# The matmuls on constants at three inner seams of a two-layer trunk are left out

## What is computed

```
def hybrid_layer(x, ...):
    h = rms_norm(x, g_mix_pre)
    proj = h @ w_in
    ...                                   # three attention branches, gated and added: mixed
    x = x + rms_norm(mixed @ w_out, g_mix_post)
    h = rms_norm(x, g_mlp_pre)
    u = jnp.square(jax.nn.relu(h @ w_up))
    return x + rms_norm(u @ w_down, g_mlp_post)
```

## Time and profile before

| what | value |
|---|---|
| median of 3 runs | 1807.53 us (1807.1 to 1808.18) |
| the profiled execution's own time | 1808.27 us |
| its span, first to last instruction | 1806.5 us |
| TensorE busy | 1763.2 us, 98% of the span |
| VectorE, ScalarE, GpSimd busy | 1057.9, 827.1, 145.0 us |
| mean granted clock of TensorE | 0.992 |
| chain that ended last | TensorE 86%, VectorE 7%, ScalarE 3% |

### The profile page before, as it was taken

One profiled execution on the slowest core, in us unless ns is written; L12 is line 12 of the kernel. 1 busy time (PEld: TensorE's weight loads), 2 busy tenths in 40 slices (PEclk: granted clock), 3 DMA queues, 4 the chain that ended last, 5 costly groups with the idle time before them and its releaser, 6 DMA issues.

```text
span 1806.5 us, 20939 instructions
## 1 busy us (share of the span) xinstructions
PE 1763.2 (98%) x8298; PEld 1450.1 (80%) x8298; DVE 1057.9 (59%) x1378; ACT 827.1 (46%) x1115; POOL 145.0 (8%) x140
## 2 busy tenths in 40 slices
PE   8999999999999999999999999999999999999996
PEld 6887888888878888888778878888888788888884
DVE  7877775654547534354487777655554664343544
ACT  7575555555345414131366755655544353231221
POOL 0111121111100000000001112111111000000000
PEclk9999999999999999999999999999999999999998
DMA  4121112222332222222221221122224132222221
GB/s 149 65 78 59 59 59 71 70 67 74 122 99 93 93 95 94 94 93 94 93 99 62 74 70 48 59 71 71 71 82 136 62 117 94 93 94 93 96 95 66
DMA packets 46609, 152.30 MB, mean 84 GB/s; under 512 B 5296, under 2 KB 7728, under 8 KB 46512
## 3 DMA queue, kind: packets, MB, share of 16 engines
q1 hardware_dynamic: 44784, 147.29, 24.5%
q10 hardware_dynamic: 1728, 3.67, 0.5%
HBM read 146.75 MB, written 4.19 MB: 84 GB/s over the span
## 4 chain that ended last, share of the span: by engine, by line
PE 86%; DVE 7%; ACT 3%; issue 2%; DMA 0%; POOL 0%; DVEq 0%; SPq 0%; ACTq 0%
PE bank L475 79%; PE bank L480 4%; PE bank L741 1%; PE bank L701 1%; DVE hf L1422 1%; DVE x L1429 1%; DVE w_lo L1378 1%; DVE h_lo L1411 1%; ACT w_hi L891 1%; DMA trig<-in_trig 0%; ACT dn L943 0%; ACT dn L941 0%; PE bank L551 0%; DVE mx L1472 0%; PE bank L496 0%
## 5 line engine op out<-in xcount | busy, mean ns | idle before, releaser
L475 PE MATMUL bank<-h_hi,w_hi 128*128 128x512 f32 x1248 | 493.3, 395 | 12.0 <-DVE h_lo L1411 10.5
L475 PE MATMUL bank<-h_hi,w_lo 128*128 128x512 f32 x1248 | 488.3, 391 | 0.0
L475 PE MATMUL bank<-h_lo,w_hi 128*128 128x512 f32 x1248 | 488.1, 391 | 0.0
L891 ACT ACTIVATE w_hi<-raw 128x1024 fp32r<-128x1024 f32 (+2 forms) x275 | 277.1, 1012 | 223.1 <-DMA raw<-in_w 222.6
L1378 DVE TENSOR_TENSOR w_lo<-raw,w_hi 128x1024 fp32r<-128x1024 f32 (+2 forms) x275 | 324.6, 1183 | 60.6 <-ACT w_hi L891 54.6
L475 PEld LDWEIGHTS bank<-h_hi,w_hi 128*128 128x128 f32 x1248 | 235.8, 189 | 66.2 <-issue 10.3
L475 PEld LDWEIGHTS bank<-h_hi,w_lo 128*128 128x128 f32 x1248 | 235.4, 189 | 49.9
L475 PEld LDWEIGHTS bank<-h_lo,w_hi 128*128 128x128 f32 x1248 | 235.7, 189 | 47.8 <-issue 1.4
L475 PE MATMUL bank<-u_hi,w_hi 128*128 128x512 f32 x512 | 203.1, 397 | 0.0
L475 PE MATMUL bank<-u_lo,w_hi 128*128 128x512 f32 x512 | 203.1, 397 | 0.0
L475 PE MATMUL bank<-u_hi,w_lo 128*128 128x512 f32 x512 | 203.1, 397 | 0.0
(11 more groups left out here) (239 smaller groups left out, 2547.4 us busy)
## 6 DMA issues: line engine op xcount, KB each, us to landing
raw<-in_w SPq DMA_DIRECT2D x257, 512.0 KB, 3.3
x<-in_x SPq DMA_DIRECT2D x16, 256.0 KB, 3.8
x_spill<-x ACTq DMA_DIRECT2D x8, 256.0 KB, 2.0
x<-x_spill SPq DMA_DIRECT2D x8, 256.0 KB, 3.4
out_y<-x SPq DMA_DIRECT2D x8, 256.0 KB, 2.0
raw<-in_w SPq DMA_DIRECT2D x8, 192.0 KB, 2.4
raw<-in_w SPq DMA_DIRECT2D x8, 128.0 KB, 2.3
raw<-in_first ACTq DMA_DIRECT2D x1, 768.0 KB, 8.8
```

The lines of the kernel that those rows point to most:

```text
L475: mm = pe.matmul(o, s, m, start=start and i == 0 and j == 0, stop=last and i == n - 1 and j == 2, skip_group_check=True)
L891: act.activation(w_hi[:, gc % RING, 0:w], raw[:, gc % RING, 0:w], ACT.Copy).then_inc(whi.sem, 1)
```

## The change

The two calls of `keep_warm(WARM)` and the constant are taken out. The warm-up at the start of the program (14 matmuls) stays. No wait is added or removed, and no other engine's program changes; TensorE issues 84 matmuls less in an execution, 28 at each of the three seams.

```
@@ -26,7 +26,6 @@
 GROUPS = D_FF // D
 
 RING = 4
-WARM = 28
 
 
 def order():
@@ -867,7 +866,6 @@
                     for t in range(KT):
                         tile(("out", t), mix_hi, mix_lo, (mix_l, 0) if t == 0 else None)
                     norm_sum(POST)
-                    keep_warm(WARM)
 
                     up(0)
                     for g in range(GROUPS):
@@ -875,8 +873,6 @@
                             up(g + 1)
                         down(g)
                     norm_sum(MPOST)
-                    if now[0] + 1 < DEPTH:
-                        keep_warm(WARM)
 
             @block.scalar
             def _(act):
```

## The result

The changed kernel took 1810.14 us (median of 20 runs, 1808.31 to 1811.63) and the kernel before 1807.31 us (median of 20, 1806.26 to 1808.49): a ratio of 1.0014 with a 95% interval of 1.0008 to 1.0020. It is slower by 2.8 us (1.4 to 3.6 by the interval). The profiled execution took 1810.25 us, 1.98 us more than that of before.

The account below looks back on a forecast made before the run. TensorE, busy 98% of the span, was taken as the bound. Constants 0.0, three slow starts of 1.95 us, less three waits of 0.60, gave + 4.05 us on 1807.53: 1811.6 us, range 1809.2 to 1814.2.

Parts of the forecast that it names:

- The constants stand beside the chain, not on it: At the three seams, constants end before the norm chain delivers input and do not slow it; removal directly gains 0.0 us.
- The clock falls at all three seams: TensorE idles about 7.6 us at each seam, so its clock is at 1.2 GHz when `three_tiles` starts.
- The price of a slow start, 1.95 us less 0.60: At each seam the first ten matmuls take 4.32 us, not 2.37; less a vanished wait, net 1.35 us.
- The wait at the fifth tile: In `three_tiles` at each seam, TensorE's 0.60 us wait for `h_lo` disappears when TensorE starts late.
- the prediction's formula: Slow-start cost at a seam with n slow matmuls: 0.30 + (n - 1) x 0.197 + 0.08 us.
- both rivals on the length of the start: At each seam: about six slow matmuls, 2.3 us in all, chance 0.10; or 14, 7.0 us in all, chance 0.13.
- I take nothing off: After the seams the whole chain moves along with TensorE, so the rest of the program swallows none of the 4.05 us.
- the row at 948.30: After the layer boundary, TensorE waits 0.91 us for VectorE work that had itself waited for TensorE.
- the fall in layer 1 lost: Rival: a clock fall in the attention goes away, saving 1.7 us, total 1809.9 us; chance 0.10.
- the opposite, one fall more, is as possible: In the attention, one extra clock fall is as possible as a lost one, and lies inside the forecast's own range.
- the rival's 1809.9: Total in us if an attention clock fall goes away: + 4.05 - 1.7 = 2.35 us; chance 0.10.
- a loss of over 0.2%: Whole kernel slower by more than 3.6 us, the least a measurement can tell from no change; chance 0.64.

Follow-up runs that it names:

- both attempts to move the pause: Against the kernel before: 42 constants at the layer boundary, 1807.43 us against 1807.79; bare boundary plus 8 constant matmuls ahead of layer 1's attention pause, 1809.26 against 1808.32.
- the last trace: Boundary constants removed and 8 constant matmuls added ahead of layer 1's attention pause, against the kernel before: 1809.26 us against 1808.32, ratio 1.0006.

## Why the prediction was right, and where it was not

**The constants stand beside the chain, not on it: right.** The 20.9 us of TensorE's time that they took are worth nothing. The chain takes 8.72 us with them and without.

**The clock falls at all three seams: right.** It does so in this kernel and at every other seam that was left bare or half bare. It fell 3.2 us after `norm_sum` at the first seam, where about 3 was said, and came back 5.8, 5.5 and 3.5 us after the first matmul of `three_tiles`, where some 4 was said.

**The price of a slow start, 1.95 us less 0.60: right in its mechanism, too small in its size.** The wait at the fifth tile went as forecast. The number of slow matmuls was the unsure term: the start's nine were taken (n in the prediction's formula; the tenth is the one in which the clock comes back), and 13, 12 and 7 came. By the prediction's own formula they give 2.14, 1.95 and 0.96 us, and 2.05, 1.90 and 0.99 were measured. Over the 13 bare or half-bare seams of six traces the mean is 1.6 us, not 1.35, so three seams cost 4.8 (4.94 in the trace of the changed kernel) in place of 4.05. Single seams came near both rivals on the length of the start, with 7 slow matmuls (six in the rival) and 13 (fourteen), but never all three of a trace.

**"I take nothing off" for the rest of the program: the step that failed.** It looked for waits that swallow the delay, and found rightly that there are none (though the row at 948.30 names no engine that ended its 0.91 us; that it waits for VectorE was concluded, not read). The traces show how exact this is. From the first matmul behind `three_tiles` at the boundary to the sum of the next norm, TensorE takes 498.05 to 498.23 us in the five traces with a fall in layer 1. It takes 496.56 to 496.69 us in the eight traces with neither a fall nor added constants there, three of them with a bare boundary, one with a half bare one, and four with a boundary at full clock. So a fall costs 1.5 us, and the slow boundary is not swallowed anywhere. The stretch between the first seam and the boundary takes 341.06 us in all fourteen traces, and the one from the third seam to the end 358.43 to 358.45.

What gave time back was not a wait but the clock's own falls in the attention. The prediction had them as a rival, at 0.10, with the fall in layer 1 lost, 1.7 us for it, and a total of 1809.9, and held that "the opposite, one fall more, is as possible". In layer 1 it was one-sided: of the kernels whose attention pause was unfilled, all four traces with a slow boundary (the changed kernel, half the constants, only the boundary bare, bare with the pause moved) had no fall there, and all five with a boundary at full clock had one. So leaving the boundary bare costs 1.6 to 2.0 us and gives 1.5 back. With 4.8 for three seams that makes + 3.3 in place of + 4.0; the median is at + 2.8, and the 0.5 between them lies within the interval and was not traced further. The fall in layer 0, ahead of the first seam, is not the change's doing: up to that seam the programs with the pause unfilled are the same, and six of their nine traces have it. That it is missing in the one trace of the changed kernel is chance.

**The total.** 1811.6 was forecast and 1810.14 measured, inside the range of 1809.2 to 1814.2, with the right sign. Two errors of opposite sign stand behind the small miss: the seams cost 0.8 us more than forecast, and 1.5 us came back in layer 1. That they cancel in part is luck. So is the closeness of the rival's 1809.9, which had the seams too cheap as well. The greater part of the chances, 0.64, had been put on a loss of over 0.2%, and it is 0.14% by the ratio.

**What stays open.** That the moment of the pause, and not the slowness before it, decides about a fall, was not shown: both attempts to move the pause moved it too little. Slowness alone is not enough to keep the clock up: ahead of the pause in layer 0 stands the slow start of the program in all nine traces with the pause unfilled, and six of them have a fall. What the traces give is an order. Counted from the last return of the clock to the end of the pause, layer 0 of the traces with a return at the start and layer 1 of those with a slow boundary fall into two groups without an overlap: no fall at 226.00 (twice), 226.32, 226.72, 226.86, 226.88 and 227.06 us; a fall at 227.32, 227.41, 227.62, 227.69, 228.24 and 228.34 us. The 227.41 and the 226.72 come from the last trace and were not used in finding the order. The five falls in layer 1 behind a boundary at full clock stand outside this order, since there the last return lies 594 to 1116 us back. Why the border lies where it does was not tried.

## What to carry to other kernels

Matmuls that compute nothing are not waste when they lie beside a chain that TensorE must wait for: count what their absence does to the clock before counting their busy time as a gain, and let them reach close to the next input (1.2 us ahead of it was enough here, and with half as many, 4.4 us ahead, the kernel was as slow as with none). Look for other pauses in the granted clock's rows, short ones too: five constants in a pause of 1.3 us of each layer were worth about as much as the 84 at the seams. And when slow stretches are removed or added, later ones may come or go with them, so time an edit together with the others and not only by its own place.

## What the runs showed of the hardware that was not expected

The clock fell at a pause of 1.27 us in a stretch of small matmuls, and stayed up over one of 1.21 us at the seams; with the pause filled it never fell there. Ten of the eleven falls came 0.1 to 1.4 us after the end of the pause, and one 0.16 us before it. After idleness of 5.7 to 8.0 us, at the start of the program and at bare seams, the slow stretch from fall to return lasted 6.8 us in some places and 10.2 us in others (534.30 to 544.54, 1428.60 to 1435.42); at the short pauses it lasted 3.4 us each time.
